# The ones products of twelve head norms per layer as two fp32r records, in place of one fp32 product

## The reference, cut to what matters

```python
def rms_norm(x, gain):
    xf = x.astype(jnp.float32)
    xf = xf * lax.rsqrt(jnp.mean(xf * xf, axis=-1, keepdims=True) + EPS)
    return (xf * gain.astype(jnp.float32)).astype(x.dtype)

    q_n = rms_norm(nq.reshape(b, t, NSA_HEADS, HEAD_DIM), nsa_q_norm)
    k_s = rms_norm(kvh(sk), nsa_k_norm[1])
    k_w = rms_norm(kvh(wk), nsa_k_norm[2])
    ...
    q_d = rms_norm(dq.reshape(b, t, DIFF_HEADS, 2, DIFF_QK_DIM), diff_q_norm)
    k_d = rms_norm(dk.reshape(b, t, DIFF_HEADS, 2, DIFF_QK_DIM), diff_k_norm)
    ...
    o_h = rms_norm(o_h, hgrn_out_norm) * jax.nn.silu(hg.reshape(b, t, HGRN_HEADS, HGRN_VAL_DIM))
```

## Time and profile before

| | |
|---|---|
| median of 3 runs | 2249.18 us (2249.03 to 2250.23) |
| span of the profiled execution, first to last instruction | 2247.3 us |
| its time by the clock of the runs | not given; the median stands 1.9 us above the span |
| granted TensorE clock | 1.00 of full speed |
| HGRN levels with head norms, layer 0 | about 485 to 551 us of the span |
| attention, layer 0 | about 551 to 690 us |
| the same stages of layer 1 | from about 1601 us |

### The profile page before, as it was taken

One profiled execution on the slowest core, in us unless ns is written; L12 is line 12 of the kernel. 1 busy time (PEld: TensorE's weight loads), 2 busy tenths in 40 slices (PEclk: granted clock), 3 DMA queues, 4 the chain that ended last, 5 costly groups with the idle time before them and its releaser, 6 DMA issues. The chain is left out here.

```text
span 2247.3 us, 29144 instructions
## 1 busy us (share of the span) xinstructions
PE 2217.1 (99%) x11560; PEld 1752.3 (78%) x11560; DVE 1185.2 (53%) x1933; ACT 915.4 (41%) x1516; POOL 155.0 (7%) x155
## 2 busy tenths in 40 slices
PE   8999999999999999999999999999999999999999
PEld 6888888876657888888878888878766578888887
DVE  6444433577775544433664444346776754444336
ACT  5232222545784322223553222235557743222234
POOL 0000000033111000000000000000431210000000
PEclk9999999999999999999999999999999999999999
DMA  5433334312112332333223233343121123333332
GB/s 190 135 101 94 96 94 141 132 59 76 55 35 81 103 103 95 100 104 99 94 94 94 94 97 93 103 149 116 57 77 45 42 90 105 94 97 105 95 98 84
DMA packets 68993, 214.41 MB, mean 95 GB/s; under 512 B 8143, under 2 KB 15311, under 8 KB 68858
## 3 DMA queue, kind: packets, MB, share of 16 engines
q1 hardware_dynamic: 59344, 189.27, 27.0%
q10 hardware_dynamic: 9514, 23.27, 3.0%
HBM read 208.30 MB, written 5.40 MB: 95 GB/s over the span
## 5 line engine op out<-in xcount | busy, mean ns | idle before, releaser
L537 PE MATMUL main<-xh,wh 128*128 128x512 f32 x1896 | 754.6, 398 | 5.7 <-DVE wl L1525 2.8
L538 PE MATMUL main<-xl,wh 128*128 128x512 f32 x1896 | 739.2, 390 | 0.0
L539 PE MATMUL main<-xh,wl 128*128 128x512 f32 x1896 | 739.0, 390 | 0.0
L1525 DVE TENSOR_TENSOR wl<-raw,wh 128x1024 fp32r<-128x1024 f32 (+2 forms) x338 | 406.8, 1204 | 350.2 <-ACT wh L1018 349.1
L1018 ACT ACTIVATE wh<-raw 128x1024 fp32r<-128x1024 f32 (+3 forms) x372 | 377.9, 1016 | 452.3 <-PE main L539 421.1
L537 PEld LDWEIGHTS main<-xh,wh 128*128 128x128 f32 x1896 | 356.1, 188 | 108.2 <-issue 26.7
L539 PEld LDWEIGHTS main<-xh,wl 128*128 128x128 f32 x1896 | 356.2, 188 | 75.2
L538 PEld LDWEIGHTS main<-xl,wh 128*128 128x128 f32 x1896 | 356.4, 188 | 73.9 <-issue 3.4
L537 PE MATMUL main<-ffh,wh 128*128 128x512 f32 x704 | 273.9, 389 | 0.0
L538 PE MATMUL main<-ffl,wh 128*128 128x512 f32 x704 | 273.9, 389 | 0.0
L539 PE MATMUL main<-ffh,wl 128*128 128x512 f32 x704 | 273.9, 389 | 0.0
(11 more groups left out here) (257 smaller groups left out, 2073.9 us busy)
## 6 DMA issues: line engine op xcount, KB each, us to landing
raw<-in_ffn_gate SPq DMA_DIRECT2D x88, 512.0 KB, 3.4
raw<-in_ffn_up SPq DMA_DIRECT2D x88, 512.0 KB, 3.5
raw<-in_ffn_down SPq DMA_DIRECT2D x64, 448.0 KB, 3.3
raw<-in_w_in_t SPq DMA_DIRECT2D x40, 512.0 KB, 3.5
raw<-in_ffn_down SPq DMA_DIRECT2D x32, 512.0 KB, 3.5
raw<-in_wout SPq DMA_DIRECT2D x24, 384.0 KB, 3.1
w<-in_cmp_w ACTq DMA_DIRECT2D x16, 512.0 KB, 4.5
raw<-in_ple_gate SPq DMA_DIRECT2D x16, 512.0 KB, 3.3
```

Of the source, the lines that this page charges most:

```text
L537: nc.tensor.matmul(out, lh, rh, start=start, stop=False, **kw)
L538: nc.tensor.matmul(out, lh, rl, start=False, stop=False, **kw)
L539: return nc.tensor.matmul(out, ll, rh, start=False, stop=stop, **kw)
L1525: nc.vector.tensor_tensor(wl[:, c % SLOTS, 0:n], raw[:, c % SLOTS, 0:n], wh[:, c % SLOTS, 0:n], ALU.subtract).then_inc(*tick("weights_lo", ...
```

## The change

Twelve of the fifteen norms get another product; `kc` and the two diff outputs keep theirs. ScalarE squares twice, once to fp32 and once rounded to fp32r (`zhi`); VectorE subtracts the second from the first, in place (`zlo` lies on the first half of `zs`, `zhi` on the second); TensorE adds two fp32r products with a rounded copy of the 0/1 matrix. As one half of the buffer is now the low part, every Square waits for the product of the norm just before. The subtraction is a new step of VectorE, placed at the head of the slot of the product in `hgrn()`, and in `attention()` between the logits of three row blocks and the scaling. The rounded matrices are made once, in `small_exponents`.

```diff
+WHOLE_SQUARES = ("kc", ("diff", 0), ("diff", 1))
...
+        sq_at = place["at"] - 4 * 2 * SEQ
+        zlo = nc.alloc_sbuf_tensor_at("zlo", [P, SEQ], F32R, offset=sq_at)
+        zhi = nc.alloc_sbuf_tensor_at("zhi", [P, SEQ], F32R, offset=sq_at + 4 * SEQ)
+        blocks_r = {"sum64": sb("sum64_r", [P, P], F32R),
+                    "sum32": nc.alloc_sbuf_tensor_at("sum32_r", [P, P], F32R,
+                                                     offset=const_at + 4 * CONST["sum32"][0])}
...
                     out = take(("head_squares", name), which)
-                    pe.wait_ge(*done("head_sq", name))
-                    nc.tensor.matmul(out[:, 0:n], const_(blocks), zs[:, slot_of(name) % 2, 0:n], start=True,
+                    if name in WHOLE_SQUARES:
+                        pe.wait_ge(*done("head_sq", name))
+                        nc.tensor.matmul(out[:, 0:n], const_(blocks), zs[:, 0, 0:n], start=True,
+                                         stop=True).then_inc(*tick("head_squares", name))
+                        return
+                    pe.wait_ge(*done("blocks_rounded", 1, layer=0))
+                    pe.wait_ge(*done("head_sq_hi", name))
+                    nc.tensor.matmul(out[:], blocks_r[blocks][:], zhi[:], start=True, stop=False)
+                    pe.wait_ge(*done("head_sq_lo", name))
+                    nc.tensor.matmul(out[:], blocks_r[blocks][:], zlo[:], start=False,
                                      stop=True).then_inc(*tick("head_squares", name))
...
                     k = len(norm_order)
-                    if k >= 2:
-                        act.wait_ge(*done("head_squares", norm_order[k - 2]))
+                    if k >= 1:
+                        act.wait_ge(*done("head_squares", norm_order[k - 1]))
                     norm_order.append(name)
                     counts.slot[(counts.layer, name)] = k
-                    nc.scalar.activation(zs[:, k % 2, 0:n], operand, ACT.Square).then_inc(*tick("head_sq", name))
+                    nc.scalar.activation(zs[:, 0, 0:n], operand, ACT.Square).then_inc(*tick("head_sq", name))
+                    if name not in WHOLE_SQUARES:
+                        nc.scalar.activation(zhi[:], operand, ACT.Square).then_inc(*tick("head_sq_hi", name))
...
+                        for n, name in enumerate(("sum64", "sum32")):
+                            V.tensor_copy(blocks_r[name][:], const_(name)).then_inc(*tick("blocks_rounded", n))
...
                             g = p * LEVELS + lev
+                            slot = g + p + 1
+                            for name in tiles_after(slot, 2):
+                                square_low(name)
+                            if p and lev == 0:
+                                square_low(("hgrn", p - 1))
                             if lev >= 0:
                                 exponents(g + 2)
...
+                def square_low(name):
+
+                    dve.wait_ge(*done("head_sq_hi", name))
+                    nc.vector.tensor_tensor(zlo[:], zs[:, 0, :], zhi[:],
+                                            ALU.subtract).then_inc(*tick("head_sq_lo", name))
...
                             logits(u, (0, 1, 2))
+                        if u == 0:
+                            square_low(("hgrn", 2))
+                        if TILE_AT.get(u - 2) in NORMED:
+                            square_low(TILE_AT[u - 2])
                         if u:
                             scale(u - 1)
```

More of the change, by code:

```diff
@@ L270, in layers @@
         wh, wl = sb("wh", [P, SLOTS, WIDE], F32R), sb("wl", [P, SLOTS, WIDE], F32R)
+        const_at = place["at"]
         const = sb("const", [P, NCONST])
@@ L1809, in hgrn @@
                                 branch_gates()
-                            slot = g + p + 1
                             for name in tiles_after(slot, 1):
```

## The result

The kernel with the change takes 2275.93 us (median of four runs, 2275.07 to 2278.89), the kernel before, run beside it, 2249.51 us. The ratio is 1.0119, 95% interval 1.0106 to 1.0131. The direction was forecast, the size was not: 16.8 us were said (2266 less 2249.2), 26.4 came, with the median at the very end of the range. The span grows from 2247.3 to 2274.3 us, by 27.0, and that is what I take apart.

What follows compares the result with a forecast made beforehand. TensorE and VectorE were taken to run side by side, TensorE a nose ahead. Per layer, HGRN +4.0 and attention +4.55 us, doubled to +17.1 on 2249.2, gave 2266 us; range 2249 to 2276.

Steps and rivals of the forecast that it cites:

- The product: From last projection record to the level behind: 0.78 us instead of 1.17, taken as 0.40 us saved per product.
- Round 1: First HGRN round: two subtractions delay score copies, so the level behind starts 1.1 us late; nq2 counted separately.
- Round 2: Second HGRN round (hgrn1, sk, wk): second Squares and subtractions delay VectorE's score copies, +3.5 us.
- The wait of VectorE at dq0: Attention: VectorE stands idle 3.8 us for ScalarE's high part, making the projection behind the transposes 1.9 us later.
- the lock-out: Attention, dk1: VectorE's subtraction stands still behind GpSimd's; bounds 0 and 1.5 us, transposes +1.95 us with it, +0.65 without.
- Failed step 1: All stretches: TensorE's granted clock stays at full speed, 2.4 GHz, so no time was added for it.
- Failed step 2: HGRN levels: nq2 falls where VectorE has slack, -0.4 us, and dk0 has room, -0.2 us, per layer.
- rival 3: HGRN levels: each of 16 subtractions stands 0.7 us behind GpSimd, up to 11 us more, 2277 us; chance 0.07.
- attention at full clock: Attention per layer: dk1 +1.95, dq0 +1.9 and dq1 +0.7 us, together +4.55 us.
- Rival 1: Whole kernel: all 24 new waits are met in time, the full 9.6 us is saved, 2239.6 us; chance 0.14.
- Rival 2: HGRN levels' bank chain is looser than read and only the attention loses: +2.7 us, 2251.9 us; chance 0.14.
- Rival 4: The twelve products: the change does not make them cheaper; its chance was put at nothing.

Runs made afterwards that it cites:

- low_on_pool: Changed kernel with only the seven norms hgrn0, hgrn1, nq0 to nq2, sk, wk split, their subtractions on GpSimd instead of VectorE: 2263.28 us.
- five_mixed_late: Changed kernel splitting only hgrn0, hgrn2, dk1, dq0, dq1, with dk1's and dq0's subtractions later and three output-projection subtractions moved behind dq1's step's fourth logits: 2253.09 us.
- dq1_alone: Changed kernel with only dq1's product split, one per layer, its subtraction ahead of the scaling; everything else as in the kernel before: 2255.07 us.
- no_sub: Changed kernel without VectorE's subtraction; the second fp32r record multiplies the high squares again, both Squares stay: 2250.42 us.
- square_twice: Kernel before with its fp32 product kept and no subtraction, but ScalarE squares twice and nobody reads the second result: 2252.30 us.
- one_square: Changed kernel with one Square straight to fp32r and no subtraction; both product records multiply that buffer: 2247.36 us.
- five_mixed_last: Splits hgrn0, hgrn2, dk1, dq0, dq1 like `five_mixed_late`, with the three moved output-projection subtractions one place further, behind the evacuations: 2249.26 us.
- hgrn_whole: Changed kernel splitting only dk0, hgrn2, dk1, dq0 and dq1; the seven other norms of the levels keep one fp32 product: 2263.51 us.
- after_mixed_late: Full changed kernel with three output-projection subtractions of VectorE moved behind the fourth logits of dq1's step: 2279.06 us.
- mixed_late: Kernel before, no split, with three output-projection subtractions of VectorE moved behind the fourth logits of dq1's step: 2247.24 us.

## Why the prediction was wrong in size

**Right.** The order of the argument: two engines side by side, the saving hidden, VectorE's place in the queue decisive. The product: 0.78 us. Round 1: +1.1 said, +0.97 measured (the level of the earlier trace rows, less the 1.88 of the start). Round 2: +3.5 said, +3.47 measured (the level of 540.32 in the earlier trace rows, less what had come by nq2's product, 3.20):

```profile
509.68 0.53 PE L676 MATMUL side<-zv 64*64 64x64 f32 x11 [0.24 <-DVE sdiag L1804]
...
547.00 0.69 PE L676 MATMUL side<-zv 64*64 64x64 f32 x32 [0.90 <-DVE sdiag L1804]
```

The +1.1 is a good number from a step that does not hold together: with 0.19 us to spare, a copy 1.0 us late makes the level 0.8 late, not 1.1. There was nothing to spare; in the kernel before this level starts 0.61 us behind the product's second record, the one behind nq0's 0.52. The wait of VectorE at dq0: 3.8 us said, and the trace has

```profile
617.57 0.69 DVE L1850 TENSOR_TENSOR zlo<-sq,zhi 128x512 fp32r<-128x512 f32 x1 [3.78 <-ACT zhi L1074]
```

with TensorE +1.7 behind it where +1.9 was said. The two copies (0.3 us), the single buffer and the extra waits cost about nothing, as taken. TensorE's waits grow by 20.2 us (all lines of the view: 24.4 before, 44.6 after), where 25 were said.

**dk1: the delay was right.** I bounded the lock-out at 0 to 1.5 us and took it. After (VectorE, GpSimd, TensorE):

```profile
572.93 1.92 DVE L1850 TENSOR_TENSOR zlo<-sq,zhi 128x512 fp32r<-128x512 f32 x1 [3.00 <-ACT zhi L1074]
```

```profile
571.94 2.37 POOL L520 TENSOR_TENSOR wl<-raw,wh 128x1024 fp32r<-128x1024 f32 x1 [14.37 <-ACT wh L1034]
```

```profile
578.34 0.50 PE L586 MATMUL side<-zhi,sum_r 128*128 128x512 f32 x1 [1.82 <-DVE small L1962]
```

The subtraction that takes 0.69 us takes 1.92, and ends 0.54 us behind GpSimd's (574.85 and 574.31), not much less than its own length: 1.2 us of delay. The Trainium skill (SBUF — State Buffer, Who interferes with whom) says that a VectorE instruction with two SBUF inputs and a GpSimd one that reads SBUF exclude each other, and that the one issued second waits; the trace agrees here, in `low_on_pool` and in `five_mixed_late`. The transposes start 1.5 us later than without hgrn2 and dk1, 1.95 was said.

**Failed step 1, the largest: "The granted clock is that of full speed (2.4 GHz) throughout, 1.00 in every stretch, also the earlier trace rows, and I leave it so."** I forecast 25 us of new waits for TensorE and kept the clock of a kernel that has few in these stages. It fell four times, at those waits; the attention loses 6.8 us by it, 2.2 in layer 0 and 4.6 in layer 1. That is most of the 9.6 us that the forecast lacks. That it comes with such waits and not with the rest of the change is shown by `dq1_alone`, where one product a layer is split, and by `no_sub`, which subtracts nothing. It should have been a term, with nothing and half the length of a stretch at half clock as its bounds. That 2275.93 us still lies inside the range to 2276 is luck: the room at its upper end was made for other errors.

**Failed step 2: "nq2 falls where VectorE has slack: -0.4" and "dk0 has room: -0.2".** They measured +0.36 and +0.6, together 3.1 us over both layers. The level behind nq2's product waits 0.7 us for ScalarE's `soff`, which stands behind an exponential, and that behind VectorE's exponents; these are late by nq2's own subtraction here. In `no_sub` and `square_twice` a like shift (+0.36, +0.34) comes from nq1's second Square, which holds up the factor that VectorE needs before them. At dk0 the subtraction runs into GpSimd's first weight chunk and takes 1.56 us, in layer 1 1.63. It is the mechanism of rival 3, at one place a layer and not at sixteen: the other fourteen subtractions in the levels take 0.68 or 0.69 us.

**Mis-sized the other way:** attention at full clock, 3.8 and 3.7 us instead of 4.55. And 1.9 us of start, most of it between executions, are in the span of 27.0 but not in my sum.

The terms close: 17.1 + 3.1 (nq2, dk0) - 0.3 (rest of the levels) - 1.6 (attention) + 6.8 (clock) + 1.9 (start) = 27.0.

**The rivals.** Rival 1 (2239.6 us) has nothing for it: even `one_square`, which adds nothing but the two copies, stays at 2247.4. So "for 24 products 9.6 us if nothing waits" is a sum that no version here got: ten of the products lie where VectorE sets the time. Rival 2 is out, as the levels lose 10.6 us alone. Rival 4 is out by the 0.23 us spacing.

**Open:** what decides whether the clock falls behind a given stall. In `five_mixed_last` the same wait of 1.95 us goes with a fall in layer 1 and with none in layer 0. The wait ahead of dk1's product goes with a fall in both layers of the changed kernel, and with none in either layer of `hgrn_whole`, where two shorter waits at dq0's transposes (0.63 us, then the 0.80 of the second row) are followed by one 0.9 us later:

```profile
572.22 0.50 PE L586 MATMUL side<-zhi,sum_r 128*128 128x512 f32 x1 [1.82 <-DVE small L1963]
...
614.67 0.24 PE L857 MATMUL side<-const,probs 64*128 64x64 f32 x1 [0.80 <-DVE small L1963]
```

So the length of a wait does not tell whether the clock falls. And no run held the clock up in the full change, so that its 6.8 us are read from starts, not from a comparison.

## What to carry to other kernels

A saving on the bound engine counts only where that engine sets the time; read it stage by stage, and expect nothing from the places where the helper engine has no gap. What is added to a queue costs first by where it stands: a two-operand VectorE step that waits for ScalarE ahead of work that TensorE needs cost 10 us here (two instructions a layer, with the clock), the same step one place later cost nothing. And when a forecast says that TensorE will wait, a fall of its clock belongs in the sum as a term, or at least in the upper end of the range.

## What the runs showed of the hardware that I had not expected

TensorE's granted clock goes to half (1.2 GHz) at waits as short as 1.23 us (`dq1_alone`) and behind pairs of 1.15 and 0.56 us (`no_sub`) or of 0.63 and 0.80 us (`hgrn_whole`), in kernels that keep it busy 98% of the time or more, and stays there for 3.4 to 10.2 us. It does not do so each time: waits of 0.75 and 1.03 us in the kernel before did not go with it, one of 1.82 us did in one kernel and not in another, one of 1.95 us in one layer and not in the other. The Trainium skill (TensorE: Matmul & The Clock Gate, A second HAM failure mode: psum-queue depth-cycling) tells of a kernel whose frequent small pauses between groups of products make the clock swing. The traces agree that the clock can fall at pauses of about a microsecond, but here they are not frequent: 1.82 us is the only wait over 0.3 us in the 12 us ahead of the fall at 580.0. Not all of it is lost: in `dq1_alone` 7 us at half clock cost 1.3 us of the stage, as a wait of 1.03 us that stands behind them in the kernel before is gone. And the pairing of GpSimd and VectorE subtractions weighed on two experiments (`after_mixed_late` and `five_mixed_late`): 1.90 us became 3.51 by a meeting that a move of some 6 us had made, while in `mixed_late` the same move missed GpSimd by 0.1 us and the three took 1.89.
